# A two-block transformer kernel: S5 input products one tile later, half of the condition blocks moved to the gate stage, the first S5 weight tile split in the FFN's tail

## The reference, cut to what matters

```python
f = swiglu(x, w1, w3, w2)                     # (silu(x @ w1) * (x @ w3)) @ w2
x = layer_norm(ALPHA * x + f, ...)            # end of the FFN stage
u = x @ w_in                                  # S5: input projection, 8 weight tiles of 128 columns
y = ...                                       # S5: scan over time with the powers of a complex pole, b and c
hid = gelu(y)
val, gate = split(hid @ w_glu)                # gate stage: 8 weight tiles of 256 columns
x = layer_norm(ALPHA * x + val * sigmoid(gate), ...)   # then the router
for l in range(2):                            # second block
    mod = silu(c) @ w_ada[l] + b_ada[l]       # 3072 numbers for each layer: the "conditions"
    h = x * (1 + scale) + shift
```

## Time and profile before

| | us |
|---|---|
| runs (median; lowest, highest) | 2575.66 (2573.46, 2578.72) |
| profiled execution, its own time | 2578.13 |
| span of the profiled execution | 2576.4 |
| PE busy in the span | 2467.8 (96%) |
| DVE busy | 1740.6 (68%) |
| ACT busy | 1044.0 (41%) |
| POOL busy | 603.0 (23%) |

### The profile page before, as it was taken

One profiled execution on the slowest core, in us unless ns is written; L12 is line 12 of the kernel. 1 busy time (PEld: TensorE's weight loads), 2 busy tenths in 40 slices (PEclk: granted clock), 3 DMA queues, 4 the chain that ended last, 5 costly groups with the idle time before them and its releaser, 6 DMA issues. The chain is left out here.

```text
span 2576.4 us, 40971 instructions
## 1 busy us (share of the span) xinstructions
PE 2467.8 (96%) x15793; PEld 2031.6 (79%) x15793; DVE 1740.6 (68%) x2854; ACT 1044.0 (41%) x1561; POOL 603.0 (23%) x481
## 2 busy tenths in 40 slices
PE   8998989999999899899999999998999998999998
PEld 7788887787878689799999999886676576767576
DVE  7944656468888743666766766676687567487666
ACT  4443233331211342455555555443344452344453
POOL 2404321430230140142333432430024001024001
PEclk9999999999999899999999999999999999999999
DMA  4321002347664552367777777843221211332121
GB/s 156 91 89 36 2 3 66 118 137 259 207 212 162 183 157 85 105 224 238 239 250 228 235 244 228 287 167 125 86 74 60 76 68 56 110 94 70 33 82 66
DMA packets 265197, 348.33 MB, mean 135 GB/s; under 512 B 23184, under 2 KB 221008, under 8 KB 264528
## 3 DMA queue, kind: packets, MB, share of 16 engines
q1 hardware_dynamic: 253872, 313.81, 37.6%
q0 software_dynamic: 5536, 17.17, 2.0%
q10 hardware_dynamic: 5632, 15.21, 1.8%
HBM read 322.83 MB, written 20.71 MB: 133 GB/s over the span
## 5 line engine op out<-in xcount | busy, mean ns | idle before, releaser
L3057 PE MATMUL ps<-x_feat_r,moe_w_hi 128*128 128x384 f32 x1408 | 405.2, 361 | 2.6 <-DVE x_feat_r L3169 2.6
L2587 DVE TENSOR_TENSOR moe_w_lo<-ring,moe_w_hi 128x2048 fp32r<-128x2048 f32 x144 | 316.8, 2201 | 130.3 <-ACT moe_w_hi L2582 130.1
L3060 PE MATMUL ps<-x_feat_r,moe_w_lo 128*128 128x192 f32 x1408 | 354.0, 251 | 0.0
L2582 ACT ACTIVATE moe_w_hi<-ring 128x2048 fp32r<-128x2048 f32 x144 | 254.8, 1770 | 97.5 <-PE ps L263 60.8
L3060 PEld LDWEIGHTS ps<-x_feat_r,moe_w_lo 128*128 128x128 f32 x1408 | 269.2, 191 | 0.3
L3057 PEld LDWEIGHTS ps<-x_feat_r,moe_w_hi 128*128 128x128 f32 x1408 | 264.3, 188 | 3.7 <-issue 3.4
L267 PE MATMUL ps<-x_free_r,ring_r 128*128 128x512 f32 x496 | 195.6, 394 | 0.0
L266 PE MATMUL ps<-ring_r,x_feat_r 128*128 128x256 f32 (+2 forms) x576 | 183.9, 319 | 0.0
L263 PE MATMUL ps<-x_feat_r,ffn_w_hi 128*128 128x512 f32 x352 | 139.7, 397 | 1.2 <-DVE ffn_w_lo L2530 1.2
L267 PE MATMUL ps<-x_feat_r,ffn_w_lo 128*128 128x512 f32 x352 | 139.5, 396 | 0.0
L266 PE MATMUL ps<-x_free_r,ffn_w_hi 128*128 128x512 f32 x352 | 138.3, 393 | 0.0
(11 more groups left out here) (654 smaller groups left out, 6401.9 us busy)
## 6 DMA issues: line engine op xcount, KB each, us to landing
ring<-in_moe_w SPq DMA_DIRECT2D x120, 1024.0 KB, 8.6
ring<-in_w_in SPq DMA_DIRECT2D x32, 1024.0 KB, 5.3
ring<-in_ffn_w SPq DMA_DIRECT2D x30, 1024.0 KB, 7.8
ring<-in_ada_t SPq DMA_DIRECT2D x48, 512.0 KB, 4.6
ring<-in_gdn_w_in SPq DMA_DIRECT2D x12, 1024.0 KB, 5.7
ring<-in_moe_w SPq DMA_DIRECT2D x24, 512.0 KB
ring<-in_s_w_glu SPq DMA_DIRECT2D x8, 1024.0 KB, 5.9
ring<-in_w_out SPq DMA_DIRECT2D x8, 1024.0 KB, 6.7
```

Source lines behind the costliest of these rows:

```text
L2582: self.prog.nc.scalar.activation(self.flat(self.hi, j % SPLITS, j), self.raw(j), ACT.Copy).then_inc(self.hi_done, 1)
L2587: self.prog.nc.vector.tensor_tensor(self.flat(self.lo, j % SPLITS, j), self.raw(j), self.flat(self.hi, j % SPLITS, j).bitcast(F32), ALU.su ...
L3057: mm = nc.tensor.matmul(out, wh[:, k, cs], both[:, k, :], start=(k == 0), stop=False)
L3060: mm = nc.tensor.matmul(out[:, 0:SLOTS], wl[:, k, cs], xg[0][:, k, :], start=False, stop=(k == KD - 1))
```

## The change

Four parts, all of them orders of work and places of work; what is computed is the same.

1. `Parameters`: one condition block per split instead of two, and only those of layer 0 (24 blocks). The `Q_AT` and `P_AT` splits are changed. `input_powers` walks its tables in another order of axes.
2. Gate stage: the 24 blocks of layer 1 are done here, four behind each of the lo parts of tiles 2 to 7, with two buffers of their own, loaded on the POOL queue.
3. The end of the FFN stage: ACT and DVE split the first S5 weight tile between token tiles 2 and 3; PE issues 11 `keep_busy` calls between `turn(2)` and `turn(3)`. The two calls at the start of S5 go, as do the splits of tile 0.
4. S5: `project(3)` stands ahead of `inputs(0)`, and what follows is one tile later; the tables of b = 3 are turned behind `outputs(0)`. ACT's, DVE's and SP's lists are changed to fit.

```diff
-    FIRST_SPLIT, PER_SPLIT = 9, 2
+    FIRST_SPLIT = 9
-    Q_AT = {9: 0, 13: 1, 17: 2, 20: 3, 23: 4, 26: 5, 29: 6, 32: 7}
-    P_AT = {11: 0, 15: 1, 19: 2, 22: 3, 25: 4, 28: 5, 31: 6, 34: 7}
+    Q_AT = {9: 0, 14: 1, 17: 2, 20: 3, 22: 4, 24: 5, 26: 6, 31: 7}
+    P_AT = {13: 0, 16: 1, 19: 2, 21: 3, 23: 4, 25: 5, 27: 6, 33: 7}
...
-        shape = [P, self.QUADS, GC, STEP]
+        shape = [P, self.QUADS, STEP, GC]
...
+def condition_block(prog, layer, n, weights, row):
+    return prog.nc.vector.scalar_tensor_tensor(out=weights, in0=weights, scalar=1.0, in1=row, op0=ALU.mult, op1=ALU.mult,
+                                               accum_out=prog.mods[:, layer, n:n + 1])
+
+def finish_conditions(prog, link, layer):
+    nc, mods, scale = prog.nc, prog.mods[:, layer, :], prog.mods[:, layer, KD:2 * KD]
+    link(nc.vector.tensor_tensor(mods, mods, prog.ada_par[:, layer, :], ALU.add))
+    link(nc.vector.tensor_scalar(scale, scale, 1.0, None, ALU.add))
...
 # S5, PE's list
-            keep_busy(prog, 7, 2)
             project(0)
             project(1)
             project(2, 0)
+            project(3)
             inputs(0)
-            project(3)
-            project(4, 1, lambda half: table_bank_free(0, half))
+            lags(0, lambda half: table_bank_free(0, half))
+            project(4)
+            project(5, 1, lag_bank_free)
             inputs(1)
-            lags(0, lambda half: table_bank_free(1, half))
-            project(5)
-            project(6, 2, lag_bank_free)
+            lags(1, lambda half: table_bank_free(1, half))
+            project(6)
+            project(7, 2, lambda half: lag_bank_free(2 + half))
             inputs(2)
-            lags(1, lambda half: table_bank_free(2, half))
-            project(7, 3, lambda half: lag_bank_free(2 + half))
-            lags(2, lambda half: table_bank_free(3, half))
+            lags(2, lambda half: table_bank_free(2, half))
             outputs(0)
-            turn_back(0, lambda half: lag_bank_free(4 + half))
+            turn_tables(3, 0, lambda half: lag_bank_free(4 + half))
+            turn_tables(3, 1, lambda half: pe.wait_ge(t_copied, 12 + half + 1))
+            turn_back(0, lambda half: table_bank_free(3, half))
...
 # S5, DVE's list
-            for n in range(3):
-                proj.split_lo(dve, n)
+            dve.sem_inc(proj.lo_done, 1)
+            proj.split_lo(dve, 1)
+            proj.split_lo(dve, 2)
             skip_diagonals()
             rotations()
             proj.split_lo(dve, 3)
             proj.split_lo(dve, 4)
+            proj.split_lo(dve, 5)
             turn_in(0)
...
 # EndNorm
+    def split_next_hi(self, act):
+        W = self.prog.weights
+        act.wait_ge(self.normed, 1)
+        W.arrived(act, NEXT, 0)
+        self.nc.scalar.activation(self.next_hi, W.flat(NEXT, 0)[0], ACT.Copy).then_inc(self.next_hi_done, 1)
+    def split_next_lo(self, dve):
+        x, lo = self.prog.weights.flat(NEXT, 0)
+        dve.wait_ge(self.next_hi_done, 1)
+        self.nc.vector.tensor_tensor(lo, x, self.next_hi.bitcast(F32), ALU.subtract)
...
 # end of the FFN stage, PE's list
                     if t:
                         by_token.turn(pe, t - 1)
+                pe.wait_ge(by_token.low_done, 2)
+                keep_busy(prog, 0, 11)
                 by_token.turn(pe, NT - 1)
...
 # ACT's list, and DVE's alike with low_parts and split_next_lo
                         end.high_parts(act, t - 1)
+                    if t == NT - 2:
+                        end.split_next_hi(act)
...
 # gate stage, DVE's list
+                def conditions(first, count):
+                    for n in range(first, first + count):
+                        if n == 0:
+                            dve.wait_ge(silu_row, 1)
+                        dve.wait_ge(cond_landed[n % 2], 16 * (n // 2 + 1))
+                        condition_block(prog, DEPTH - 1, n, cond_w[:, n % 2, :], cond_row).then_inc(cond_used, 1)
+                each = COND_BLOCKS // (2 * LAST)
                 for c in range(LAST):
                     tiles.split_lo(dve, 2 * c + 2)
+                    conditions(2 * c * each, each)
                     for t in range(NT):
                         add(c, t, c * NT + t)
...
                     tiles.split_lo(dve, 2 * c + 3)
+                    conditions((2 * c + 1) * each, each)
+                dve.wait_ge(cond_used, COND_BLOCKS)
+                finish_conditions(prog, link, DEPTH - 1)
                 spread(0)
...
 # gate stage, POOL's list
+                pool.dma_start(cond_row, inp["ada_c"]).then_inc(row_landed, 16)
+                for n in range(COND_BLOCKS):
+                    if n >= 2:
+                        pool.wait_ge(cond_used, n - 1)
+                    pool.dma_start(cond_w[:, n % 2, :], inp["ada_t"][DEPTH - 1, n * P:(n + 1) * P, :]
+                                   ).then_inc(cond_landed[n % 2], 16)
```

More of the change, by code:

```diff
@@ L1797, in blocks_at @@
     def blocks_at(self, split):
-        first = (split - self.FIRST_SPLIT) * self.PER_SPLIT
-        return range(max(first, 0), min(max(first + self.PER_SPLIT, 0), DEPTH * self.BLOCKS))
+        n = split - self.FIRST_SPLIT
+        return range(n, n + 1) if 0 <= n < COND_BLOCKS else ()
     def load_block(self, sp, n):
-        if n < DEPTH * self.BLOCKS:
-            layer, i = divmod(n, self.BLOCKS)
-            sp.dma_start(self.weights[n % 2], self.inp["ada_t"][layer, i * P:(i + 1) * P, :]
-                         ).then_inc(self.weights_landed[n % 2], 16)
+        if n < COND_BLOCKS:
+            sp.dma_start(self.weights[n % 2], self.inp["ada_t"][0, n * P:(n + 1) * P, :]).then_inc(self.weights_landed[n % 2], 16)
     def loads(self, sp, split):
@@ L1974, in condition @@
             dve.wait_ge(self.weights_landed[n % 2], 16 * (n // 2 + 1))
-            nc.vector.scalar_tensor_tensor(out=self.weights[n % 2], in0=self.weights[n % 2], scalar=1.0, in1=self.row,
-                                           op0=ALU.mult, op1=ALU.mult, accum_out=mods[:, layer, i:i + 1]
-                                           ).then_inc(self.weights_used, 1)
-            if n == DEPTH * self.BLOCKS - 1:
+            condition_block(self.prog, 0, n, self.weights[n % 2], self.row).then_inc(self.weights_used, 1)
+            if n == COND_BLOCKS - 1:
                 dve.wait_ge(self.weights_used, n + 1)
                 dve.wait_ge(self.bias_landed, 16)
-                link(nc.vector.tensor_tensor(mods, mods, self.prog.ada_par, ALU.add))
-                for l in range(DEPTH):
-                    scale = mods[:, l, KD:2 * KD]
-                    m = nc.vector.tensor_scalar(scale, scale, 1.0, None, ALU.add)
-                link(m)
+                finish_conditions(self.prog, self.linked(dve), 0)
+COND_BLOCKS = 3 * D // P
+def condition_block(prog, layer, n, weights, row):
[5 more added lines that the diff above has]
+    link(nc.vector.tensor_scalar(scale, scale, 1.0, None, ALU.add))
 def load_turned(sp, u_dram, u_blk, f, landed):
@@ L2644, in __init__ @@
         names = ("gamma_landed", "beta_landed", "norm_link", "var_ready", "sd_ready", "centred", "normed", "turned", "x_hi_done",
[L2645 removed]
+                 "measured", "low_done", "next_hi_done")
         (self.gamma_landed, self.beta_landed, self.norm_link, self.var_ready, self.sd_ready, self.centred, self.normed,
[L2647 removed]
+         self.turned, self.x_hi_done, self.measured, self.low_done, self.next_hi_done) = (st.counter(n) for n in names)
         self.link = None
+        self.next_hi = prog.split_scratch[:, 0, 0:D]
+    def split_next_hi(self, act):
[7 more added lines that the diff above has]
+        self.nc.vector.tensor_tensor(lo, x, self.next_hi.bitcast(F32), ALU.subtract)
     def loads(self, sp):
@@ L2886, in vector @@
                         end.low_parts(dve, t - 1)
+                    if t == NT - 2:
+                        end.split_next_lo(dve)
                 end.low_parts(dve, NT - 1)
@@ L3425, in router @@
         sig = prog.sbuf("s5_sig", [P, 2, UP_COLS], own)
+        cond_row = prog.sbuf("cond_row", [P, D], own)[:, :]
+        cond_w = prog.sbuf("cond_w", [P, 2, D], own)
         turned_logits = prog.sbuf("moe_turned", [EXPERTS, NT, P], own)
@@ L3459, in router @@
             pick, token, spot = gather
+            row_landed, silu_row, cond_used = st.counter("row_landed"), st.counter("silu_row"), st.counter("cond_used")
+            cond_landed = [st.counter(f"cond_landed_{i}") for i in range(2)]
             late = slice(0, SLOTS - P)
@@ L3695, in _ @@
                 tiles.split_hi(act, 1)
+                act.wait_ge(row_landed, 16)
+                nc.scalar.activation(cond_row, cond_row, ACT.Silu).then_inc(silu_row, 1)
                 for c in range(LAST):
```

46 lines of the change are left out of this document (20 added, 26 removed).

## The result

| | before | after |
|---|---|---|
| median of the runs, us | 2576.0 (2573.46 to 2578.72) | 2588.86 (2583.64 to 2592.25) |
| span of the profiled execution, us | 2576.4 | 2588.3 |

The changed kernel is slower: ratio 1.0049, 95% interval [1.0037, 1.006]. I had forecast 2572.7, a gain of 3.0 us; it came out 12.9 us slower, beyond the upper end of my range (2581).

A forecast was written before the change was run, and what follows sets the result against it. PE, busy 96% of the span, was taken to bound the kernel. Terms -6.1 + 0.65 - 4.95 + 7.4 = -3.0 from the median 2575.66 gave 2572.7 us, called "no change"; range 2566 to 2581.

The forecast's parts named there:

- FFN (-6.1): FFN: stalls of 2.9 and 1.6 us at first w2 tiles vanish, 1.6 of slow products too; -6.1 us.
- the slow time behind the first stall: FFN: 4.85 us of products at mean clock 0.65 would take 3.2 at full clock, -1.6 us.
- Border (+0.65, then -1.5): FFN to S5: first S5 product 0.65 us later, then 1.5 us won if the clock holds.
- S5 (-4.95): S5: 90.05 us from first product to `outputs(1)` become 85.1, start's 1.5 included; a 5.3 us stall at `project(3)`.
- Rival D: S5: DVE stall at `project(3)` eats what the later `inputs` give, 2577.6 us; chance 0.08.
- Gate stage (+7.4): Gate stage: block-load waits on DVE make the norm's first add later, 1057.1 against 1049.70; +7.4 us.
- a group then takes 1.15 + 3.85 + 1.15 + 1.15 = 7.3 us, 2.7 of it waiting: Gate stage: in each group of four blocks only the third waits, its load 3.85 us from issue to landing.
- the 2 that I had named as a sign of being wrong: Gate stage: third blocks' waits under 2 or over 3.5 us would show the prediction wrong.
- rival B: Gate stage: block loads land late, 2579.9 us, or 2584.7 if a pair's second load comes 0.8 later; chance 0.18.
- stay ahead of PE: Gate stage: lo parts 3 to 6 come before PE needs them; PE stalls only at tile 7, 3.0 us.
- My upper bound for the stage, +16: Gate stage: worst cost of the moved blocks, +16 us, with a landing of 4.9 us.
- Rival C: Gate stage: POOL writes descriptors only when DVE lets it, costing 4.5 us, 2577.2; chance 0.1.

The follow-up runs named there:

- e10: The kernel before plus only the border's part: first S5 tile split in the FFN's tail, eleven keep_busy calls there, none at S5's start; 2580.36 us, 1.0008.
- e4: The changed kernel with all 48 condition blocks back in the FFN, two a split, none in the gate stage; 2572.72 us, 0.9976 of the kernel before.
- e7: The changed kernel with the third weight tile's lo part ahead of the last doubling of the rotations; 2582.91 us, 1.0007 of the kernel before.
- e9: The kernel before with only the new order of S5, nothing of the FFN, border or gate stage; 2574.88 us, 0.9986.
- e12: The changed kernel, two buffers, gate-stage loads behind the first two cut to 128 KB from 512; 2576.46 us, 0.9989 of the kernel before.

## Why the prediction was wrong

**FFN (-6.1), right.** Measured 6.6 between e10 and the changed kernel; no stall is left at the first w2 tiles, part two's last product comes 6.5 us sooner, and the denser tables did not break their cover. Of the 6.6, by e4, the blocks gave 3.85 and the tables the rest. One term in it is not firm: 1.6 of it was the slow time behind the first stall, and whether there is any differs between executions (last section).

**Border (+0.65, then -1.5), right in its first half.** e10 has +0.48, and `turn(3)` starts 7.1 us behind the first of the eleven calls (7.3 forecast). The 1.5 us to be won behind it came as 0.7 alone, and in the whole change were paid back at `project(3)`.

**S5 (-4.95), mechanism right, 1.2 us too much.** The stall that I named, at `project(3)`, for the lo part behind the rotations, is there with 5.50 us (5.3 forecast), and both stalls for u tiles are gone. The term that was too small is the slow stretch behind the stall: 1.5 us in the forecast, 2.6 by the PE time that e7 saves. Rival D is out: e9 gives 5.8 us by the order alone. That the sum came so near is in part luck, since the order alone gave 2.3 us more than my terms for it (4.95 less the start's 1.5), and the border took 2.0 back.

**Gate stage (+7.4), wrong: +20.6.** The failed step is "a group then takes 1.15 + 3.85 + 1.15 + 1.15 = 7.3 us, 2.7 of it waiting", with "blocks 0 and 1 of a group are there". The waits of the changed kernel by the place of the block in its group:

| block of the group | waits in six groups, us | sum | forecast |
|---|---|---|---|
| third | 2.95, 3.50, 2.57, 2.83, 1.64, 2.83 | 16.3 | 16.2 |
| fourth | 1.06, 2.00, 4.17, 1.06, 0.99, 1.10 | 10.4 | 0 |
| first and second | 0.27 and 0.27 (group 3), 1.10 (group 5) | 1.6 | 0 |

In sum the third block's wait is right to the tenth, which is in part luck: the single waits go from 1.64 to 3.50 us, and 1.64 is below the 2 that I had named as a sign of being wrong. I had let the fourth block start as soon as the third was done, as though its load, issued 1.15 us behind the other, landed 1.15 us behind it. It lands about a microsecond later than that in four groups, 2.0 in the second and 4.2 in the third. In e12, with a quarter of the bytes, the fourth block waits in one group only, by 0.42 us; so the microsecond goes with the bytes of the two loads that are under way together. The two larger waits fall together with the load of a weight tile of 1024 KB that SP issued at 995.35 and at 1006.66 and that took 8.0 and 7.3 us to land; groups four to six, with 1.06, 0.99 and 1.10, have no such load beside them. The stretch from issue to landing of the fourth block's load in group three, and in group four (columns as above; the last but one is the share of the DMA engines' time):

```profile
1006.66 0.37 SPq L104 DMA_DIRECT2D ring<-in_s_w_glu  x1
```
```profile
1007.59:1015.27 7.68, 7.68 (x66) 7.68 (x66) 1.23 (x2) 0.00 (x0) 1.05 (x2) 1.00 0.92 337
1026.83:1031.65 4.82, 4.82 (x35) 4.82 (x35) 1.23 (x2) 0.06 (x1) 1.06 (x2) 0.79 0.61 218
```

No run moves the weight tiles away, so for these two waits the cause is a coincidence seen twice and not a test. I had written that "the stage moves little else"; it moves four such tiles.

That the fourth load is late is the second half of my rival B ("if the second load of a pair shares the DMA engines with the first and comes 0.8 later"), which I had priced at 4.8 us and which cost 10.4; its first half, that the third block's load is late as well, did not happen. And where two lo parts follow each other without adds between (tiles 3 and 4, 5 and 6), the 2.2 us of a lo part are no full cover for a load of 4: 1.6 us in groups three and five.

With this the 13.2 us are accounted for along DVE's list, which the stretch follows to its end. It reaches the first group 16.1 us behind the first product (16.2 forecast), spends 25.1 us between and behind the groups (25.4 forecast), and 57.1 us in the six groups, where I had 43.8. Of these 13.3 us more, 12.1 are waits. The rest is some 0.08 us for each of the 15 blocks that wait: a block that does not wait begins that much before the one ahead of it has ended (977.93 against 978.01).

The path was wrong as well: with longer groups the lo parts do not "stay ahead of PE". PE stalls at tile 5 already, by 6.31 us. I had written that this would show the prediction wrong. My upper bound for the stage, +16, was too low, since it scaled only the third block's landing. The chance of about 0.1 that I left beyond the range's upper end does not fit the 0.16 that I gave to more than 2580.8 either.

Rival C is out. POOL issues a load 0.30 us behind the end of the block that frees the buffer, while the next block runs on DVE (the first block ends at 976.79 + 1.22 = 978.01, the second runs until 979.15):

```profile
978.31 0.53 POOL L3717 DMA_DIRECT2D cond_w<-in_ada_t  x1 [16.95 <-DVE cond_w L1981]
```

A block beside the issues takes 1.22 us, as those without. The lock that the Trainium skill describes ("SBUF — State Buffer", section "SBUF: two separate sides") does not show in these rows; I had cited it too broadly, since by that section a VectorE operation with two SBUF inputs is locked only against a GpSimd operation that reads SBUF.

The rule on landing that I had cited from the Trainium skill ("DMA: Bandwidth & Descriptors", section "Anatomy of one DMA — SWDGE (gpsimd) path": 2.0 us plus bytes/436e3) gives, as an estimate, 2.3 us for e12's 128 KB, against 2.4 measured in the middle, and 3.2 for 512 KB, against 3.5 at the least and 4.2 in the middle. With its figure the forecast would have been further off.

**Behind the gate stage.** I had counted nothing there. The norm gave back 1.5 us. The last stretch is 4.1 us longer with the same 7860 matmuls, and over all 14 kernels of this study it takes 1480 to 1487 us without following any edit, so I put no part of it down to the change. The timed medians (12.9) and the stages' balance (9.2 without the last stretch and without the start's 1.4) leave a difference of 3.7 us open.

## What to carry to other kernels

Moving work under an engine's idle time needs two checks: that the time is idle, and that the work can get its data at the pace at which it runs. With k buffers, the pace of a streamed operation is k per round trip (end of use, issue, landing), and the landing to take is that of loads issued in pairs, not of a single one; here, with 5.1 to 9.2 us from one block of a group to the next in the same buffer, 2 buffers cost 20 us, and 4 cost 0.7. What else is loaded in the stage belongs in the landing too. An edit that lets an engine arrive sooner at the next wait is worth nothing until what it waits for is moved as well: the border's part, worth nothing alone and by the differences above a loss with the new S5 order, is to be tried together with the earlier lo part. No run here has the earlier lo part without it.

## What the runs showed of the hardware

The same stall is not always followed by a slow clock. The stall of 2.88 us at the first w2 tile of the kernel before (585.45) stands in e9 with 2.89 (584.34), and all that comes ahead of it is the same. The 5 us around its end and behind it, in the one and in the other (columns as above):

```profile
585.00:590.00 5.00, 4.55 (x14) 3.57 (x15) 5.00 (x7) 1.91 (x1) 3.85 (x2) 0.69 0.33 93
```
```profile
585.00:590.00 5.00, 5.00 (x24) 4.05 (x23) 5.00 (x5) 1.86 (x1) 4.07 (x2) 1.00 0.55 120
```

A mean of 0.69 means that part of it ran at the lower level of 1.2 GHz, 1.00 that all ran at 2.4; e9's second stall comes 1.55 us sooner for it. In e10, with the same code up to there, the stall of 2.88 us is followed by slow products again (0.43 us from start to start). A term for "slow products behind a stall" is a chance, not a certainty. The same lottery is in the last 1480 us. In the kernel with the split moved earlier (e7) the experts and the second block took this:

```profile
1100.00:2587.10 1487.10, 1439.11 (x7860) 1159.55 (x7860) 1010.62 (x1784) 684.39 (x1020) 341.80 (x253) 0.99 0.45 144
```

That is 7.0 us more than before, 6.2 of it PE busy for longer with the same number of matmuls. So a single profile of this kernel tells a far stage's time to within some 7 us, and the stretch near an edit to a few tenths where no low clock falls in: the gate stretch without waits read 77.71 to 77.76 in five executions.
